# Constant matmuls in two of TensorE's gaps, and ScalarE's weight copy behind the second root at four layer boundaries

## The chip, the cores and the metric

One core of a Trainium2 chip runs the kernel. The metric is the device time of one execution in microseconds. Engines are named as in the profile: PE is TensorE (PEld its weight loads), DVE VectorE, ACT ScalarE, POOL GpSimd, SP SyncE, which issues the DMAs.

## What is computed

Three layers run over 512 tokens of 1024 features, all in float32. The first is a convolution block: two projections around a gated depthwise convolution of 31 taps and a layer norm. The second is latent attention with 8 heads. The third mixes a gated delta rule and a sliding window. Each is followed by a feed-forward part. The part of the reference that matters here is what stands between two parts, in the first two layers:

```python
for layer in range(DEPTH):
    ...
    h = h + rms_norm(m, mix_post_g[layer])
    f = squared_relu_mlp(rms_norm(h, ffn_pre_g[layer]), w_ff1[layer], w_ff2[layer])
    h = h + rms_norm(f, ffn_post_g[layer])
```

So between two projections stand a norm of the output, an addition to the residual, and a second norm. And in the convolution block:

```python
u = jax.nn.silu(layer_norm(u, ln_g, ln_b))
return u @ w_pw2 + b_pw2
```

## The kernel before

Features lie on the 128 partitions, the 512 tokens along the free axis; 1024 features are 8 tiles. Every engine has its own list of instructions, written out by hand, and runs it in that order; semaphores connect them. Nothing is scheduled by a planner.

**Weights** come as a stream of numbered chunks of 128 x 2048 float32. For chunk c SP loads `wraw`, ACT copies it to `whi` in a rounded form (`head(c)`, line 626), and the rest `wlo = wraw - whi` is made either by POOL (`rest(c)`, line 535) or, for the chunks named in `BY_DVE`, by VectorE (`weights_low(c)`, line 1279). Activations are split the same way into a high part (`xh`, `hh`) and a low part (`xl`, `hl`). A projection then takes three matmuls in place of one: high x high, high x low, low x high (line 2113 for 512 columns, line 2136 for half the tokens, 256 columns). TensorE starts chunk c when `lo_ready` has reached c + 1 and the pair of PSUM banks is free. SP loads chunk c when `lo_ready` has reached c - 1.

**The beginning.** ACT squares the input, VectorE adds the squares up, TensorE sums them over the partitions with a matmul of ones (line 2204), ACT makes the root (lines 641 and 642), and VectorE and ACT make `xh` and `xl` tile by tile (lines 1266, 654, 1259), for which TensorE waits. In the convolution block POOL adds products of taps (line 542), VectorE adds others (line 1437), TensorE others (`taps`, line 2227), and a sigmoid gate (ACT line 769, VectorE line 1416) stands before each tile's taps.

**The layer norm ahead of the second projection** (`pw2`): TensorE sums tiles and squares (lines 2249 and 2254), then ACT and VectorE make the root, SiLU, `hh` (line 827) and `hl` (line 1514) tile by tile. The projection takes each tile as it comes.

**A boundary** (`boundary(i, ...)` on PE, DVE and ACT, for i = MIX0, FFN0, MIX1, FFN1; the fifth boundary, OUT, has code of its own) joins the last four chunks of one part (the last is `last`) and the first two of the next (`last + 1`, `last + 2`). The tokens are taken in two halves, so that the second half's projection hides the first half's norms. TensorE's order is: chunks last-1 and last for half 0, the same for half 1, then last+1 and last+2 for half 0, then both for half 1. Within chunk last+1, half 0, after its first four operand tiles, it does the last sums of squares of half 1:

```python
project_half(last + 1, half, hi, lo, need=need(0, half),
             midway=((0, 4), lambda: post_sums(i, 1, (3, 4))) if half == 0 else None)
```

These sums wait for ACT's last square `post_square(3, 1)` (line 668), which waits for VectorE's evacuation `evac(3, 1)` (line 1536, 1540 or 1581). The sums release ACT's root `post_root_of(1)` (Ln on line 673, Exp on 674). `high(0, j, half)` (line 679) makes the high part of the next operand, `low` (line 1304) on VectorE the low part, after `scale` (line 1293) and `add` (line 1299). VectorE's order around chunk last+2 is:

```python
for j in range(4, DT):
    low(0, j, 0)
weights_low(last + 2)
if i == FFN0:
    for j in range(DT):
        low(1, j, 0)
dve.wait_ge(post_root, 2 * i + 2)
```

and behind it come the scales, additions and low parts of half 1. At FFN0 chunk last+2 has a second operand (`hh`, `hl`). POOL makes the rest of chunk last+3 onwards.

Of the kernel before, what the change touches and what calls it, by code (L numbers as in the profile page):

```python
# [24 lines left out]
P = 128  # L25
# [3 lines left out]
DT = D // P  # L29
# [110 lines left out]
def build(nc, A, out):  # L140
    ctx = ExitStack()
    with ctx:
        def sb(name, shape, dt=F32):
            return ctx.enter_context(nc.sbuf_tensor(name, shape, dt))

        def sem(name):
            return ctx.enter_context(nc.semaphore(name))
# [15 lines left out]
        K = sb("K", [P, N_CONST])  # L163
        PV = sb("PV", [P, N_VEC])
        small = sb("small", [P, N_COLS])
        ps = ctx.enter_context(nc.psum_tensor("ps", [P, 8, SEQ], F32))
# [15 lines left out]
        ident, ones, half_ones = map(const, ("ident", "ones", "half_ones"))  # L182
# [12 lines left out]
        pool_sum, TAP_BANK, ODD_BANK = (E[:, 0, :], E[:, 1, :]), (6, 7), (4, 5)  # L195
# [115 lines left out]
        pair_free = [sem("pair_free_even"), sem("pair_free_odd")]  # L311
# [72 lines left out]
        def weights(c):  # L384

            if c < DT and c // 2 % 2:
                return lent[c % 2][:, 0:CW], lent[c % 2][:, CW:2 * CW]
            return whi[:, c % 2, :], wlo[:, c % 2, :]

        def weights_free(eng, c, h=0):  # L390

            if c >= DT + 2:
                eng.wait_ge(chunk_done, h * 2 + (c - 1))
            elif c >= 4:
                eng.wait_ge(chunk_done, c - 3)

        def pair(c):
            return 2 * (c % 2)
# [5 lines left out]
        def emptied(eng, c, h=0):  # L404

            eng.wait_ge(pair_free[c % 2], h + (c // 2 + 1))
# [202 lines left out]
        def _(act):  # L609
            steps = [0]  # L610

            def step(ins):

                steps[0] += 1
                ins.then_inc(act_step, 1)
                act.wait_ge(act_step, steps[0])

            def head(c, h=0):

                if isinstance(h, int) and c + 2 * h >= N_CHUNK:  # L620
                    return
                p = c % 2
                w = WIDTH[c + 2 * h] if isinstance(h, int) else CW
                act.wait_ge(raw_loaded[p], h * 16 + 16 * (c // 2 + 1))
                weights_free(act, c, h)
                act.activation(weights(c)[0][:, 0:w], wraw[:, p, 0:w], ACT.Copy).then_inc(hi_ready, 1)  # L626
# [32 lines left out]
            def boundary(i):  # L659
                last = LAST[i]  # L660

                def post_square(m, half):
                    if half:
                        emptied(act, last - 3 + m)
                    else:
                        act.wait_ge(evac_half, 2 * i + m - 1)
                    s = 2 * (m - 2)
                    act.activation(sq_half[:, s:s + 2, :], Y[:, 2 * m:2 * m + 2, TOK[half]],
                                   ACT.Square).then_inc(post_sq, 1)

                def post_root_of(half):
                    act.wait_ge(post_summed, 2 * i + half + 1)
                    step(act.activation(POST[half], POST[half], ACT.Ln, scale=1.0 / D, bias=eps_rms))
                    act.activation(POST[half], POST[half], ACT.Exp, scale=-0.5).then_inc(post_root, 1)

                def high(s, j, half):
                    (name, at, hi, _), hi_sem, _, _ = pre_norms(i)[s]
                    act.wait_ge(resid_half, DT * i + DT // 2 * half + j // 2 + 1)
                    act.activation(hi[:, j, TOK[half]], resid[:, j, TOK[half]], ACT.Copy,
                                   scale=vec(name, at + j)).then_inc(hi_sem, 1)  # L680

                def pre_squares(half):
                    for m in range(DT // 2):
                        act.wait_ge(resid_half, DT * i + DT // 2 * half + m + 1)
                        act.activation(Z[:, 2 * m:2 * m + 2, TOK[half]], resid[:, 2 * m:2 * m + 2, TOK[half]],
                                       ACT.Square).then_inc(pre_sq, 1)

                for m in range(2):
                    c = last - 3 + m
                    head(c + 2)  # L690
                    emptied(act, c)
                    if m:
                        act.wait_ge(post_added, 3 * i + 1)
                    for n in range(2):
                        act.activation(SQ[:, n, :], Y[:, 2 * m + n, :], ACT.Square).then_inc(post_sq, 1)
                    if m == 0 and i == MIX0:
                        act.wait_ge(rel_summed, 1)
                        act.activation(rel_rows, ps[0:SW_H, 6, 0:RELW], ACT.Copy).then_inc(rel_copied, 1)
                act.wait_ge(post_added, 3 * i + 2)
                post_square(2, 0)  # L700
                post_square(3, 0)
                post_root_of(0)
                head(last + 1)
                post_square(2, 1)
                for j in range(6):
                    high(0, j, 0)
                head(last + 2)
                post_square(3, 1)
                for j in range(6, DT):
                    high(0, j, 0)  # L710
                post_root_of(1)
                if i == FFN0:
                    for j in range(DT):
                        high(1, j, 0)
                pre_squares(0)
                for j in range(DT):
                    high(0, j, 1)
                if i == FFN0:
                    for j in range(DT):
                        high(1, j, 1)  # L720
                    head(last + 3)
                pre_squares(1)
# [34 lines left out]
            c0 = START["pw1"]  # L757
# [72 lines left out]
            c0 = START["pw2"]  # L830
# [39 lines left out]
            c0 = START["latent"]  # L870
# [233 lines left out]
            for t in range(TT):  # L1104
                par = t % 2
                act.wait_ge(rows_summed, t + 1)
                c0 = COLS["state_decay"][0] + 8 * par
# [962 lines left out]
        def _(pe):  # L2070
# [19 lines left out]
            def project(c, hi, lo, h=0, k_tiles=DT, k0=0, need=None, second=None, second_need=None,  # L2090
                        paired=True, midway=None, hooks={}, start=True, bank=None):

                if start:
                    start_chunk(c, h)
                p = c % 2
                bank = 2 * p if bank is None else bank

                order = ([(n, k) for k in range(k_tiles) for n in range(2)] if need and paired else
                         [(n, k) for n in range(2) for k in range(k_tiles)])
                for n, k in order:  # L2100
                    if midway and (n, k) == (1, 0):
                        midway()
                    if (n, k) in hooks:
                        hooks[(n, k)]()
                    if n and second:
                        hi, lo = second
                    if need and n == 0:
                        need(k)
                    if second_need and n == 1:
                        second_need(k)  # L2110
                    w = slice(k * 2 * P + n * P, k * 2 * P + (n + 1) * P)
                    for q, (wt, xt) in enumerate(passes(hi, lo, *weights(c))):
                        ins = pe.matmul(ps[:, bank + n, :], wt[:, w], xt[:, k0 + k, :],  # L2113
                                        start=k == 0 and q == 0, stop=k == k_tiles - 1 and q == 2)
                    if isinstance(h, int) and c == N_CHUNK - 1 and (n, k) == (0, k_tiles - 1):
                        ins.then_inc(last_half, 1)
                ins.then_inc(chunk_done, 1)
# [64 lines left out]
            def operand(name):  # L2182
                return lambda k: pe.wait_ge(split_done, SPLIT0[name] + k + 1)

            def project_tokens(c, k_tiles, n_out, need=None, hooks={}):
# [13 lines left out]
                                            start=k == 0 and q == 0, stop=k == k_tiles - 1 and q == 2)  # L2199
                ins.then_inc(chunk_done, 1)  # L2200

            pe.wait_ge(ones_loaded, 16)
            pe.wait_ge(squares_added, 1)
            pe.matmul(ps[:, SUMS, :], ones, Y[:, 0, :], start=True, stop=True).then_inc(squares_summed, DT)
            c0 = START["pw1"]
            ready = operand("mix0_pre")

# [57 lines left out]
            rest_sum(DT - 1).then_inc(rest_summed, 1)  # L2265
            rest_square(DT - 1)
            c0 = START["pw2"]
            project(c0, hh, hl, need=operand("ln"))

            def distance_bias():  # L2270
# [9 lines left out]
            def ffn(layer):  # L2280
# [11 lines left out]
                with pe.Fori(1, FF_BLOCKS - 1) as b:  # L2292
# [12 lines left out]
                    bank=LATENT_BANK)  # L2305
# [281 lines left out]
            for t in range(TT):  # L2587
# [40 lines left out]
                for lv in range(1, 6):  # L2628
# [4 lines left out]
                    for g in range(2):  # L2633
                        pe.wait_ge(level_x, 10 * t + 2 * lv + g - 1)
                        for i in range(2):
# [3 lines left out]
                                            start=True, stop=True)  # L2639
# [11 lines left out]
                    for g in range(2):  # L2651
# [3 lines left out]
                        for i in range(2):  # L2655
                            hp = slice((2 * g + i) * P, (2 * g + i + 1) * P)
                            ip, up = slice(i * P, (i + 1) * P), slice(HALF + i * P, HALF + (i + 1) * P)
                            if lv < 5:
                                ins = pe.matmul(ps[:, LEVEL_Q[g], ip], inverse[g][:, up], level_mask[:, hp],  # L2659
                                                start=True, stop=True)  # L2660
                            else:
                                ins = pe.matmul(ps[:, LEVEL_Q[g], up], level_mask[:, hp], inverse[g][:, up],
                                                start=True, stop=True)
# [201 lines left out]
```

## Time and profile before

| | |
|---|---|
| median of 3 runs | 1952.64 us (1952.09 to 1953.35) |
| the profiled execution's own time | 1951.87 us |
| its span, first to last instruction | 1950.1 us |
| mean granted TensorE clock | 0.999 |
| busy: PE, PEld | 1909.4 us (98%), 1592.3 us (82%) |
| busy: DVE, ACT, POOL | 824.0, 783.3, 681.5 us |
| the longest line: L2113 on PE | 61% of the chain that ended last |

Matmuls are pipelined, so a record's duration is longer than the distance to the next: one counts distances between starts. A float32 matmul has two records (a matmul of rounded operands one). The chain that ended last is followed back from the last instruction; what is on it sets the end. The four boundaries lie around 190 to 242, 546 to 603, 754 to 807 and 1111 to 1163 us.

### The profile page before, as it was taken

The page shows a single profiled execution, that of the slowest core. Times are in us where ns is not written, and L with a number is a line of the kernel's source. Part 1 is how long each engine was busy: PE and PEld are TensorE (multiplying, and loading weights), DVE is VectorE, ACT ScalarE, POOL GpSimd, SP SyncE. Part 2 cuts the span into 40 slices and gives each one's busy share as a digit, 9 for nine tenths or more (in the row PEclk, how much of TensorE's full clock was granted, in tenths as well). Part 3 has the DMA queues.
Part 4 walks back from the last instruction along what each step waited for, and adds up shares of the span by engine and source line. Part 5 has one row for each costly group of instructions (what it writes and reads, how often), then busy time and mean ns, then how long its engine had stood idle before and what let it go on. Part 6 is the DMA issues. An engine that isn't in the chain of part 4 may idle for free.

```text
span 1950.1 us, 24716 instructions
## 1 busy us (share of the span) xinstructions
PE 1909.4 (98%) x9804; PEld 1592.3 (82%) x9804; DVE 824.0 (42%) x1366; ACT 783.3 (40%) x1179; POOL 681.5 (35%) x217
## 2 busy tenths in 40 slices
PE   6998999999999999999999999999999999999999
PEld 4666988888897779888888897778898898888887
DVE  5996621111266474612111377756552352122122
ACT  6665432222345462523222256755454342122221
POOL 3993043434301210243343313222123403434442
PEclk9999999999999999999999999999999999999999
DMA  5211264222221211332322312111122322222322
GB/s 191 68 42 66 76 122 102 101 89 105 89 90 49 81 44 47 106 108 87 108 104 90 108 56 87 66 49 60 44 82 92 114 82 107 96 99 87 108 81 92
DMA packets 30510, 169.40 MB, mean 87 GB/s; under 512 B 3755, under 2 KB 6092, under 8 KB 13516
## 3 DMA queue, kind: packets, MB, share of 16 engines
q1 hardware_dynamic: 30412, 168.01, 25.8%
q8 instruction: 72, 1.18, 0.3%
q14 instruction: 26, 0.21, 0.0%
HBM read 162.22 MB, written 5.77 MB: 86 GB/s over the span
## 4 chain that ended last, share of the span: by engine, by line
PE 88%; DVE 5%; ACT 4%; POOL 2%; issue 1%; DMA 1%; SPq 0%; POOLq 0%; DVEq 0%; ACTq 0%
PE ps L2113 61%; PE ps L2136 8%; PE ps L2474 4%; PE ps L2541 3%; PE ps L2227 2%; POOL wlo L535 1%; PE ps L2638 1%; PE ps L2198 1%; ACT whi L626 1%; PE ps L2659 1%; DVE wlo L1279 1%; PE ps L2363 1%; PE ps L2380 1%; PE ps L2381 1%; PE ps L2398 1%
## 5 line engine op out<-in xcount | busy, mean ns | idle before, releaser
L535 POOL TENSOR_TENSOR wlo<-wraw,whi 128x2048 fp32r<-128x2048 f32 (+4 forms) x138 | 570.5, 4134 | 1192.1 <-ACT whi L626 1160.3
L626 ACT ACTIVATE whi<-wraw 128x2048 fp32r<-128x2048 f32 (+4 forms) x154 | 268.1, 1741 | 372.1 <-PE ps L2113 348.8
L2113 PE MATMUL ps<-xh,whi 128*128 128x512 f32 x980 | 386.7, 395 | 5.8 <-DVE xl L1259 4.3
L2113 PE MATMUL ps<-xl,whi 128*128 128x512 f32 x980 | 382.0, 390 | 0.0
L2113 PE MATMUL ps<-xh,wlo 128*128 128x512 f32 x980 | 381.9, 390 | 0.0
L2113 PE MATMUL ps<-hh,whi 128*128 128x512 f32 x752 | 295.3, 393 | 5.9 <-DVE hl L1514 5.7
L2113 PE MATMUL ps<-hh,wlo 128*128 128x512 f32 x752 | 293.1, 390 | 0.0
L2113 PE MATMUL ps<-hl,whi 128*128 128x512 f32 x752 | 293.1, 390 | 0.0
L2113 PEld LDWEIGHTS ps<-xh,whi 128*128 128x128 f32 x980 | 184.4, 188 | 48.3 <-issue 8.7
L2113 PEld LDWEIGHTS ps<-xl,whi 128*128 128x128 f32 x980 | 184.4, 188 | 39.3 <-issue 1.9
L2113 PEld LDWEIGHTS ps<-xh,wlo 128*128 128x128 f32 x980 | 184.3, 188 | 38.5
L2113 PEld LDWEIGHTS ps<-hh,whi 128*128 128x128 f32 x752 | 141.5, 188 | 37.7 <-issue 8.5
L2113 PEld LDWEIGHTS ps<-hl,whi 128*128 128x128 f32 x752 | 141.6, 188 | 30.0 <-issue 1.0
L2113 PEld LDWEIGHTS ps<-hh,wlo 128*128 128x128 f32 x752 | 141.4, 188 | 29.6
L848 ACT ACTIVATE hh<-Z 128x1024 fp32r<-128x1024 f32 x32 | 33.9, 1059 | 214.7 <-DVE Z L1560 212.0
L1560 DVE SCALAR_TENSOR_TENSOR Z<-ps,RS 128x1024 f32<-128x1024 f32 x28 | 34.3, 1224 | 183.2 <-PE ps L2113 183.2
L1437 DVE SCALAR_TENSOR_TENSOR ps<-Z,PV,ps 128x512 f32<-128x512 f32 x140 | 96.2, 751 | 8.4 <-ACT ps L801 4.1
L2136 PE MATMUL ps<-hh,whi 128*128 128x256 f32 x336 | 97.8, 291 | 0.0
L2136 PE MATMUL ps<-hh,wlo 128*128 128x256 f32 x336 | 95.1, 283 | 0.0
L2136 PE MATMUL ps<-hl,whi 128*128 128x256 f32 x336 | 95.0, 283 | 0.0
L2136 PE MATMUL ps<-xh,whi 128*128 128x256 f32 x304 | 88.1, 290 | 1.6 <-DVE xl L1304 1.6
L2136 PE MATMUL ps<-xl,whi 128*128 128x256 f32 x304 | 86.0, 283 | 0.0
(351 smaller groups left out, 2958.0 us busy)
## 6 DMA issues: line engine op xcount, KB each, us to landing
wraw<-stream SPq DMA_DIRECT2D x132, 1024.0 KB, 4.8
wraw<-stream SPq DMA_DIRECT2D x12, 768.0 KB, 4.1
wraw<-stream SPq DMA_DIRECT2D x6, 384.0 KB, 3.2
resid<-x SPq DMA_DIRECT2D x4, 512.0 KB, 5.1
wraw<-stream SPq DMA_DIRECT2D x8, 256.0 KB, 3.0
branch_scratch<-RS SPq DMA_DIRECT2D x8, 256.0 KB, 2.0
wraw<-stream SPq DMA_DIRECT2D x4, 512.0 KB, 3.7
rel_scratch<-E SPq DMA_DIRECT2D x8, 192.0 KB, 8.9
```

The source lines that it names most:

```text
L535: pool.tensor_tensor(lo[:, 0:w], wraw[:, p, 0:w], hi[:, 0:w], ALU.subtract).then_inc(lo_ready, 1)
L626: act.activation(weights(c)[0][:, 0:w], wraw[:, p, 0:w], ACT.Copy).then_inc(hi_ready, 1)
L848: act.activation(hh[:, 2 * j:2 * j + 2, :], t, ACT.Square)
L1279: dve.tensor_tensor(wlo[:, p, 0:w], wraw[:, p, 0:w], whi[:, p, 0:w], ALU.subtract).then_inc(lo_ready, 1)
L1437: dve.scalar_tensor_tensor(out=NT[:, at:at + 1, :] if last else acc, in0=x, scalar=tap(k, j, h), in1=acc, op0=ALU.mult, op1=ALU.add).then_ ...
L1560: ins = dve.scalar_tensor_tensor(out=t, in0=ps[:, 2 * p:2 * p + 2, :], scalar=0.0, in1=rs_pair(), op0=ALU.max, op1=ALU.mult)
L2113: ins = pe.matmul(ps[:, bank + n, :], wt[:, w], xt[:, k0 + k, :], start=k == 0 and q == 0, stop=k == k_tiles - 1 and q == 2)
L2136: ins = pe.matmul(half_bank(c, half)[:, n, :], wt[:, p, w], xt[:, k, TOK[half]], start=(n, k, q) == (0, 0, 0), stop=(n, k, q) == (1, DT - ...
L2198: ins = pe.matmul(dst, xt[:, k, t * P:(t + 1) * P], wt[:, p, k * n_out:(k + 1) * n_out], start=k == 0 and q == 0, stop=k == k_tiles - 1 an ...
L2227: ins = pe.matmul(ps[:, TAP_BANK[at], :], w, shifted(k, j, h), start=n == 0, stop=n == len(diags) - 1)
L2474: ins = pe.matmul(ps[:, slot_bank(s), :], wt[:, c % 2, w], xt[:, m // 3, :], start=m == 0, stop=m == 3 * DT - 1)
L2541: ins = pe.matmul(ps[:, bank, :], wt[:, p, w0 + k * P:w0 + (k + 1) * P], xt[:, k0 + k, :], start=r in (0, 24), stop=r == last)
```

## The change

1. In ACT's `boundary`, `head(last + 2)`, which stood between the high parts 0 to 5 of half 0 and `post_square(3, 1)`, now stands behind that square, the high parts 6 and 7 and `post_root_of(1)`. This holds for all four boundaries.
2. On TensorE a new function `stay_awake` multiplies the identity by 256 columns of constants in float32, into a bank that nobody reads at the time: six times behind the first sum (bank 7), eleven times ahead of the second projection (the first bank of its pair, which the projection's own start overwrites). Ahead of the eleven stands a wait that the projection had anyway (`pair_free[0]`).

```diff
                 post_square(2, 1)
                 for j in range(6):
                     high(0, j, 0)
-                head(last + 2)
                 post_square(3, 1)
                 for j in range(6, DT):
                     high(0, j, 0)
                 post_root_of(1)
+                head(last + 2)
                 if i == FFN0:
                     for j in range(DT):
                         high(1, j, 0)
...
+            def stay_awake(bank, times):
+
+                for n in range(times):
+                    pe.matmul(ps[:, bank, 0:2 * P], ident, K[:, 0:2 * P], start=True, stop=True)
+
             pe.wait_ge(ones_loaded, 16)
             pe.wait_ge(squares_added, 1)
             pe.matmul(ps[:, SUMS, :], ones, Y[:, 0, :], start=True, stop=True).then_inc(squares_summed, DT)
+            stay_awake(TAP_BANK[1], 6)
             c0 = START["pw1"]
...
             rest_sum(DT - 1).then_inc(rest_summed, 1)
             rest_square(DT - 1)
             c0 = START["pw2"]
+            pe.wait_ge(pair_free[0], DT // 2)
+            stay_awake(pair(c0), 11)
             project(c0, hh, hl, need=operand("ln"))
```

ACT's order at the first boundary (L626 is the weight copy, L668 the square, L679 the high parts, L673 and L674 the root, L685 squares for the next norm):

```order
 L668 ACTIVATE SQ<-Y 128x512
 L679 ACTIVATE xh<-resid,PV 128x256 x6
-L626 ACTIVATE whi<-wraw 128x2048
 L668 ACTIVATE SQ<-Y 128x512
 L679 ACTIVATE xh<-resid,PV 128x256 x2
 L673 ACTIVATE ps<-ps,small 128x256
 L674 ACTIVATE ps<-ps 128x256
+L626 ACTIVATE whi<-wraw 128x2048
 L685 ACTIVATE Z<-resid 128x2x256 x4
 L679 ACTIVATE xh<-resid,PV 128x256 x8
```

The copy went past five instructions; the order on VectorE, POOL and SP is the same as before.

TensorE's order ahead of the second projection, before (L2249 and L2254 are the sums, L2113 the projection):

```order
L2249 MATMUL ps<-Y,K 128x512
L2254 MATMUL ps<-SQ,K 128x512
L2249 MATMUL ps<-Y,K 128x512
L2254 MATMUL ps<-SQ,K 128x512
L2113 MATMUL ps<-hh,whi 128x512
L2113 MATMUL ps<-hl,whi 128x512
```

and in the changed kernel (the same sums are lines 2255 and 2260 there):

```order
L2255 MATMUL ps<-Y,K 128x512
L2260 MATMUL ps<-SQ,K 128x512
L2205 MATMUL ps<-K 128x256 x11
L2113 MATMUL ps<-hh,whi 128x512
L2113 MATMUL ps<-hl,whi 128x512
```

The eleven constant matmuls stand between the last sum and the projection's first matmul, which waits for the first `hl`.

## Rows read from the trace of the kernel before

**Rows 1.** The page: the chain that ended last, by engine.
```profile
PE 88%; DVE 5%; ACT 4%; POOL 2%; issue 1%; DMA 1%; SPq 0%; POOLq 0%; DVEq 0%; ACTq 0%
```
**Rows 2.** Waits of PE, whole run: line, released by: us in total, times, longest.
```profile
PE ps L2113 <- DVE hl L1514: 5.7, 1, 5.7
...
PE ps L2150 <- ACT SQ L668: 2.6, 4, 0.8
```
**Rows 3.** The chain in order of time, first 240 us: start, us, what.
```profile
33.18 4.55 POOL hh L535
...
49.77 3.67 PE ps L2227 x8
```
**Rows 4.** PE in order of time, the beginning: start, us, what, [idle before <-releaser].
```profile
18.22 0.77 PE L2113 MATMUL ps<-xh,whi 128*128 128x512 f32 x1 [4.33 <-DVE xl L1259]
...
34.53 3.67 PE L2227 MATMUL ps<-Z 128*128 128x512 f32 x8 [0.88 <-DVE Z L1416]
```
**Rows 5.** Stretches around the second gap: length, busy us of each engine, then PEclk.
```profile
162.20:164.40 2.20, 0.00 (x0) 0.00 (x0) 1.44 (x3) 2.16 (x4) 2.20 (x3) 1.00 0.88 372
164.40:165.30 0.90, 0.00 (x0) 0.01 (x1) 0.82 (x2) 0.87 (x3) 0.48 (x1) 0.77 0.04 18
165.30:168.30 3.00, 2.98 (x7) 2.42 (x8) 2.72 (x5) 2.32 (x4) 0.00 (x0) 0.50 0.00 0
```
**Rows 6.** PE in order of time, the second projection.
```profile
165.32 0.77 PE L2113 MATMUL ps<-hh,whi 128*128 128x512 f32 x1 [5.72 <-DVE hl L1514]
...
168.39 0.39 PE L2113 MATMUL ps<-hl,whi 128*128 128x512 f32 x1
...
177.47 0.39 PE L2113 MATMUL ps<-hh,wlo 128*128 128x512 f32 x1
```
**Rows 7.** The chain: two float32 matmuls of 256 columns (four records).
```profile
204.61 0.87 PE ps L2150 x4
```
**Rows 8.** DVE in order of time: the first and the last of the eight hl.
```profile
164.48 0.69 DVE L1514 TENSOR_TENSOR hl<-ps,hh 128x512 fp32r<-128x512 f32 x1 [0.84 <-ACT hh L827]
...
174.69 0.69 DVE L1514 TENSOR_TENSOR hl<-ps,hh 128x512 fp32r<-128x512 f32 x1 [0.61 <-ACT hh L827]
```
**Rows 9.** ACT in order of time, first boundary.
```profile
216.60 1.90 ACT L626 ACTIVATE whi<-wraw 128x2048 fp32r<-128x2048 f32 x1
218.40 0.61 ACT L668 ACTIVATE SQ<-Y 128x512 f32<-128x512 f32 x1
218.92 0.89 ACT L679 ACTIVATE xh<-resid,PV 128x256 fp32r<-128x256 f32 x2
220.24 0.45 ACT L673 ACTIVATE ps<-ps,small 128x256 f32<-128x256 f32 x1 [0.42 <-PE ps L2150]
...
221.00 2.18 ACT L685 ACTIVATE Z<-resid 128x512 f32<-128x512 f32 x4
```
**Rows 10.** DVE in order of time, first boundary.
```profile
216.47 0.87 DVE L1536 TENSOR_SCALAR Y<-ps,PV 128x256 f32<-128x256 f32 x2
...
218.15 0.69 DVE L1299 TENSOR_TENSOR resid<-resid,Y 128x512 f32<-128x512 f32 x1
...
220.34 2.29 DVE L1279 TENSOR_TENSOR wlo<-wraw,whi 128x2048 fp32r<-128x2048 f32 x1
```
**Rows 11.** PE, first boundary: the sums, and the first matmul of chunk last+2.
```profile
219.07 1.13 PE L2150 MATMUL ps<-SQ,K 128*128 128x256 f32 x4 [0.80 <-ACT SQ L668]
...
222.90 0.28 PE L2136 MATMUL ps<-xh,whi 128*128 128x256 f32 x1
```
**Rows 12.** ACT's second Ln and DVE's low part of chunk last+2, second boundary.
```profile
576.62 0.45 ACT L673 ACTIVATE ps<-ps,small 128x256 f32<-128x256 f32 x1 [0.42 <-PE ps L2150]
...
576.63 2.28 DVE L1279 TENSOR_TENSOR wlo<-wraw,whi 128x2048 fp32r<-128x2048 f32 x1
```
**Rows 13.** PE, second boundary: first matmul of chunk last+2, and a later wait.
```profile
579.29 0.28 PE L2136 MATMUL ps<-xh,whi 128*128 128x256 f32 x1
...
590.16 0.39 PE L2136 MATMUL ps<-xh,whi 128*128 128x256 f32 x1 [0.61 <-DVE xl L1304]
```

## The prediction

> **What bounds the kernel now.** I read the page's chain by engine first, then TensorE's list of waits, then the order in time around the places that the change touches. The chain by engine says that TensorE is the bound nearly everywhere: it has 88% of it [rows 1]. So a microsecond is won or lost only where TensorE stands still or runs slowly. Its list of waits is short. The two entries that bear on this change are the 5.7 us ahead of the second convolution projection (waiting for hl) and 2.6 us in four pieces, all before the sums of the squares at a boundary (L2150, waiting for ACT's square at L668) [rows 2].
>
> **Constants in the first gap: nothing.** Six fp32 matmuls of 256 columns now stand between the first sum and the first projection. TensorE waited 4.33 us there, and the projection began at 18.22 us [rows 4]. Two such matmuls took 0.87 us at the full clock, so 0.435 each [rows 7]; at half clock 0.87 each, 5.2 us in all. The first sum ended 4.33 before 18.22, at 13.9, so at worst the six end near 19.1, 0.9 us after the projection could have begun. At best they raise the clock early and the first chunk ends some 0.7 us sooner. Neither reaches the end of the kernel: the chain there does not run over TensorE but over ACT and POOL (POOL's weight rest at 33.18 us and its products) and joins TensorE only at 49.77 us [rows 3], and TensorE itself still stands 0.88 us before its first taps at 34.53, for VectorE's gate [rows 4]. That gate comes after an ACT sigmoid that stands behind ACT's tap weights and weight copy. I take 0, with bounds of -0.7 and +0.1.
>
> **Constants in the second gap: a gain of 0.7 us.** After the last sum of squares TensorE is idle for 5.72 us and begins the projection at 165.32 [rows 6]. The granted clock was 1.00 from 162.2 to 164.4, 0.77 from 164.4 to 165.3, and 0.50 from 165.3 to 168.3: it fell near the end of the idle stretch from 2.4 to 1.2 GHz [rows 5]. The first seven matmuls took 3.07 us (165.32 to 168.39) and the next forty are 0.227 apart (168.39 to 177.47) [rows 6], so slowness cost 3.07 - 7 x 0.227 = 1.5 us. Now eleven constant matmuls fill 11 x 0.435 = 4.8 us; the last sum had ended at 165.32 - 5.72 = 159.6, so they are through at 164.4, 0.9 us before the first hl is there. They delay nothing, and an idle stretch of 0.9 us is less than the 4.8 us that passed at full clock. The whole 1.5 is not won, because ACT and VectorE hand over hl tile by tile: the last one begins at 174.69 and takes 0.69, so it is there at 175.38. The first was there at 165.17 (164.48 + 0.69) [rows 8], and TensorE began at 165.32: a handover of 0.15. So the last tile's six matmuls (6 x 0.227 = 1.36) start at 175.5 at the earliest and end at 176.9, against 177.47 + 0.23 = 177.7 before. That is 0.8; a restart after a short wait costs some 0.1, so I take 0.7. Bounds: 0 (the clock falls all the same) and 1.5. Everything behind hangs on this projection, so the gain carries on.
>
> The Trainium skill (TensorE: Matmul & The Clock Gate, "Part 1: The HAM clock gate") says that the number of slow matmuls varies between runs of one kernel, with 6 to 14 measured. This trace shows 7; with the rule's upper figure the gain would be up to 1.4 us larger and the sum +5.5 instead of +6.9. I go by the trace.
>
> **The weight copy at the four boundaries: a loss of 7.6 us.** In each boundary ACT's copy for chunk last+2 (1.90 us) moves behind the second half's last square, the last two high parts and the second root. I follow the first boundary.
>
> Before: copy at 216.60, square at 218.40, high parts at 218.92, Ln at 220.24, and the instruction behind Ln and Exp at 221.00, 0.76 after Ln [rows 9]. TensorE stood 0.80 us for that square, until 219.07 [rows 11].
>
> Now: VectorE's last evacuation ends at 217.34 (216.47 + 0.87) [rows 10], so the square runs at 217.37. TensorE gets to its sums at 218.27 and does not stand: 0.80 won there. High parts 6 and 7 need VectorE's addition, which ends at 218.84 (218.15 + 0.69) [rows 10]; their 0.89 less the usual overlap of 0.08 keeps ACT until 219.68. The sums, 0.80 earlier, release Ln from 219.44 (219.07 to 220.24 was 1.17). So Ln is at 219.68, and the copy starts at 220.44 and ends at 222.34.
>
> What is late next: VectorE's own order is unchanged, and it wanted this copy at 220.34 for the low part of chunk last+2, 2.29 us long [rows 10]. It now stands until 222.37, **2.03 us**, and behind it on VectorE stand all the scales, additions and low parts of the second half. The low part is ready at 222.37 + 2.29 = 224.66, and TensorE needs 0.15 from there. Before, TensorE took up that chunk at 222.90 [rows 11], 0.27 after the low part was there (222.63). So it has only 0.12 us of cover: it arrives 0.8 earlier, waits some 2.6, and begins at 224.8, **1.9 us later** than before. The 0.80 won is already inside this.
>
> The other three boundaries have the same rows with a wait of 0.61 instead of 0.80 ((2.6 - 0.8) / 3 from rows 2). There the sums, not the high parts, release Ln, so it comes 0.61 earlier, and the copy ends at old Ln - 0.61 + 0.76 + 1.90, which is 2.05 after the old Ln. VectorE wanted it 0.01 after the old Ln (576.63 against 576.62) [rows 12], so with a 0.03 handover it is 2.07 late. TensorE's cover is 579.29 - 578.91 - 0.15 = 0.23 [rows 12, 13], so 1.8 later at the second of the feed-forward boundaries and at the attention's. At the first feed-forward boundary TensorE afterwards stood three times for VectorE's low parts (the last 0.61 us at 590.16) [rows 13]; it is VectorE's delay that counts there: 2.07.
>
> ACT's queue: behind the copy stand the squares of the sum and the second half's high parts, which wait for VectorE's additions anyway and are later by what VectorE is later. SP's load of chunk last+4 waits for the same low part, so its DMA is issued 2 us later; its copy comes only after chunks that are later by as much. POOL works on chunk last+3 onwards, off the same TensorE signal as before.
>
> Sum: 1.9 + 2.07 + 1.8 + 1.8 = 7.6, less 0.7, is +6.9. The profiled execution took 1951.87 us (span 1950.1), so 1958.8; the median of the runs shown, 1952.64, is 0.77 above that execution, so I say **1959.5 us**. Its own range is 1957.3 to 1961.9: 0.3 for each boundary, the bounds of the second gap, and 0.7 of scatter.
>
> **Rivals.**
> (a) *The clock falls in the new waits.* TensorE now stands some 2.6 us at each boundary. If that takes the clock to half, each boundary pays what the slow stretch above cost, 1.5 us, four times: 1965.4. Against it: the clock was still 1.00 at 162.2 to 164.4, after more than 2.6 us without a matmul [rows 5]. The Trainium skill (same page, "A second HAM failure mode: psum-queue depth-cycling") has a kernel in which even small repeated idle stretches let the clock swing; in this trace TensorE stood 0.80 us before 219.07 and then did two sums and 24 matmuls of 256 columns in the 3.83 us to 222.90 [rows 11], while seven of 512 columns took 3.07 us at half clock, so the trace does not show that here. 7%.
> (b) *The copy is covered after all.* If VectorE's or TensorE's next need for chunk last+2 lay more than 2 us behind, the change would win all waits: 0.7 + 0.8 + 3 x 0.61 = 3.3, giving 1949.3. That decides at a cover of 2.0 us; the rows show VectorE with none and TensorE with 0.12 to 0.23. 6%.
> (c) *The boundary loses, but half.* If the copy ran about 1 us earlier than I work out (ACT waiting less for the sums, or the 1.90 us overlapping what stands ahead), each boundary would lose 1 us: 1952.64 + 4 - 0.7 = 1955.9. 5%.
> (d) *The constants do nothing for the clock.* Then the sum is +7.6, inside my range. It is part of the forecast.
> The forecast itself has 80%; 2% is left for what I have not thought of.
>
> **How the numbers follow.** A measurement of this kernel tells about 0.2% (3.9 us) from no change, so slower means above 1956.5. The forecast and (a) lie there: 0.87. Rivals (b) and (c) are no change: 0.11. Faster by over 0.2% needs more than all waits won: 0.02. The range runs from 1957.0 to 1964.0: the forecast's own, and above it a clock that falls in one or two of the boundaries.
>
> **What the next profile would show.** TensorE's list of waits: no entry for L2150 behind ACT's square, and in its place four of some 2.6 us at the first matmul of chunk last+2, released by VectorE's wlo at L1279. VectorE: that instruction preceded by about 2 us of idle time on ACT's whi. Before the second projection: about 0.9 us idle instead of 5.72, granted clock 1.00 behind it. Its first matmul is no earlier than before. I am wrong if VectorE does not stand there, if TensorE takes chunk last+2 up without a wait, or if the granted clock behind a boundary's wait reads 0.50.

## The result, and the profile after

| | before | after |
|---|---|---|
| median | 1953.34 us (1952.09 to 1953.97, 6 runs) | 1961.42 us (1959.27 to 1962.12, 6 runs) |
| ratio, 95% interval | | 1.0041 [1.0031, 1.0051] |
| profiled execution: its time, span | 1951.87, 1950.1 us | 1959.27, 1957.5 us |
| VectorE, ScalarE, POOL busy | 824.0, 783.3, 681.5 us | 823.8, 784.1, 681.6 us |

The change costs 8.1 us. The three engines beside TensorE do as much work as before, and the span is 7.4 us longer, so the time is TensorE's, standing still or running slowly. TensorE's list of waits in the changed kernel (line, released by: us in total, times, longest) says where:

```profile
PE ps L2136 <- DVE wlo L1279: 9.2, 4, 2.3
...
PE ps L2136 <- DVE xl L1304: 1.8, 3, 0.6
PE ps L2113 <- DVE hl L1514: 1.0, 1, 1.0
```

The entry of the square at the boundaries [rows 2] is gone, and in its place stand four waits of 2.3 us for VectorE's low part of the weights. The wait before the second projection went from 5.7 to 1.0 us, because constants fill the rest.

ScalarE in order of time at the first boundary (to be held against [rows 9]):

```profile
214.47 0.91 ACT L679 ACTIVATE xh<-resid,PV 128x256 fp32r<-128x256 f32 x2 [3.30 <-DVE resid L1299]
216.04 0.63 ACT L668 ACTIVATE SQ<-Y 128x512 f32<-128x512 f32 x1 [0.67 <-DVE Y L1536]
217.55 0.91 ACT L679 ACTIVATE xh<-resid,PV 128x256 fp32r<-128x256 f32 x2 [0.87 <-DVE resid L1299]
218.36 0.42 ACT L673 ACTIVATE ps<-ps,small 128x256 f32<-128x256 f32 x1
218.82 0.37 ACT L674 ACTIVATE ps<-ps 128x256 f32<-128x256 f32 x1
219.10 1.91 ACT L626 ACTIVATE whi<-wraw 128x2048 fp32r<-128x2048 f32 x1
```

VectorE there [rows 10], the last low parts of the operand and then the low part of the weights:

```profile
217.43 1.67 DVE L1304 SCALAR_TENSOR_TENSOR xl<-resid,PV,xh 128x256 fp32r<-128x256 f32 x4
221.04 2.29 DVE L1279 TENSOR_TENSOR wlo<-wraw,whi 128x2048 fp32r<-128x2048 f32 x1 [1.94 <-ACT whi L626]
```

And TensorE [rows 11, 13], the first matmul of chunk last+2 at the four boundaries:

```profile
223.39 0.38 PE L2136 MATMUL ps<-xh,whi 128*128 128x256 f32 x1 [2.29 <-DVE wlo L1279]
...
581.48 0.38 PE L2136 MATMUL ps<-xh,whi 128*128 128x256 f32 x1 [2.29 <-DVE wlo L1279]
...
791.85 0.51 PE L2136 MATMUL ps<-xh,whi 128*128 128x256 f32 x1 [2.29 <-DVE wlo L1279]
...
1151.41 0.38 PE L2136 MATMUL ps<-hh,whi 128*128 128x256 f32 x1 [2.29 <-DVE wlo L1279]
```

ScalarE's copy starts 0.74 us after Ln. VectorE had nothing that it might do first and stood 1.94 us. TensorE stood 2.29.

**Where 7.4 us come from.** I take the distances between the same points of the two profiles. From the start of the second projection to the first boundary's chunk last+2: 57.58 us before (165.32 to 222.90), 58.70 after (164.69 to 223.39), +1.1. To the last wait of the second boundary: 367.26 before (to 590.16), 369.27 after (592.66), +2.0. To the third boundary's chunk: 197.58 before (787.74), 199.19 after, +1.6. To the fourth's: 356.40 before (1144.14), 359.56 after, +3.2. That is 7.9. The changed kernel's profile was 0.6 ahead already where the second projection begins (164.69 against 165.32), and 0.1 came at the end. Two of these points in the profile of before:

```profile
787.74 0.28 PE L2136 MATMUL ps<-xh,whi 128*128 128x256 f32 x1
...
1144.14 0.28 PE L2136 MATMUL ps<-hh,whi 128*128 128x256 f32 x1
```

and the last wait of the second boundary after:

```profile
592.66 0.39 PE L2136 MATMUL ps<-xh,whi 128*128 128x256 f32 x1 [0.60 <-DVE xl L1304]
```

The odd one is the last, which holds 3.2 where the same wait cost 1.6 to 2.0 elsewhere (1.8 at the first boundary, without the 0.7 of the constants). The stretches of 3.0 us behind the four waits (length, busy us of each engine, then PEclk):

```profile
223.40:226.40 3.00, 3.00 (x25) 3.00 (x26) 2.93 (x7) 0.93 (x3) 0.00 (x0) 1.00 0.60 180
581.50:584.50 3.00, 3.00 (x25) 3.00 (x26) 3.00 (x8) 2.87 (x6) 0.00 (x0) 1.00 0.32 87
791.90:794.90 3.00, 3.00 (x14) 3.00 (x15) 2.93 (x7) 0.97 (x3) 0.00 (x0) 0.51 0.62 191
1151.40:1154.40 3.00, 2.99 (x25) 2.99 (x26) 2.93 (x7) 0.91 (x2) 0.00 (x0) 1.00 0.52 177
```

Behind the third wait TensorE ran at 0.51 of its clock, 1.2 GHz, and did 14 matmuls where it did 25 behind the others: 11 x 0.12 = 1.3 us lost in this window; the clock came back only at about 795.4, which makes it 1.5. So my rival (a) happened as well, at one boundary of this execution. How often it happens is what the experiments settle.

### The profile page after: what moved, and what is told of

Read it like the earlier page. It is cut to its first block, busy times and chain, and to the rows that moved or that the text cites. A ratio compares the mean times of both kernels' runs of the same rounds, so it can differ in the third digit from the quotient of the medians.

```text
span 1957.5 us, 24784 instructions
## 1 busy us (share of the span) xinstructions
PE 1918.3 (98%) x9838; PEld 1598.4 (82%) x9838; DVE 823.8 (42%) x1366; ACT 784.1 (40%) x1179; POOL 681.6 (35%) x217
## 4 chain that ended last, share of the span: by engine, by line
PE 87%; DVE 6%; ACT 4%; POOL 2%; issue 1%; DMA 0%; SPq 0%; POOLq 0%; DVEq 0%; ACTq 0%
PE ps L2113 61%; PE ps L2136 8%; PE ps L2482 4%; PE ps L2549 3%; PE ps L2233 2%; POOL wlo L535 1%; DVE wlo L1279 1%; ACT whi L626 1%; PE ps L2646 1%; PE ps L2198 1%; PE ps L2667 1%; PE ps L2371 1%; DVE Y L1293 1%; PE ps L2388 1%; PE ps L2389 1%
## 5 line engine op out<-in xcount | busy, mean ns | idle before, releaser
L626 ACT ACTIVATE whi<-wraw 128x2048 fp32r<-128x2048 f32 (+4 forms) x154 | 268.2, 1741 | 372.3 <-PE ps L2113 348.1
L2113 PE MATMUL ps<-xh,whi 128*128 128x512 f32 x980 | 386.4, 394 | 1.8 <-POOL wlo L535 0.8
L2113 PE MATMUL ps<-xh,wlo 128*128 128x512 f32 x980 | 381.5, 389 | 0.0
L2113 PE MATMUL ps<-xl,whi 128*128 128x512 f32 x980 | 381.5, 389 | 0.0
L2113 PE MATMUL ps<-hh,whi 128*128 128x512 f32 x752 | 294.8, 392 | 1.2 <-DVE hl L1514 1.0
L2113 PE MATMUL ps<-hh,wlo 128*128 128x512 f32 x752 | 292.7, 389 | 0.0
L2113 PE MATMUL ps<-hl,whi 128*128 128x512 f32 x752 | 292.7, 389 | 0.0
L2113 PEld LDWEIGHTS ps<-xh,whi 128*128 128x128 f32 x980 | 184.0, 188 | 43.8 <-issue 3.0
L2113 PEld LDWEIGHTS ps<-xl,whi 128*128 128x128 f32 x980 | 184.0, 188 | 39.0 <-issue 1.9
L2113 PEld LDWEIGHTS ps<-xh,wlo 128*128 128x128 f32 x980 | 183.9, 188 | 38.6
L2113 PEld LDWEIGHTS ps<-hh,whi 128*128 128x128 f32 x752 | 141.1, 188 | 33.4 <-issue 3.3
L2113 PEld LDWEIGHTS ps<-hl,whi 128*128 128x128 f32 x752 | 141.2, 188 | 29.8 <-issue 1.0
L2113 PEld LDWEIGHTS ps<-hh,wlo 128*128 128x128 f32 x752 | 141.1, 188 | 29.5
```

## The experiments

My theory: the loss is the time by which the copy is late for VectorE, and on top of it the clock, where it falls in TensorE's new waits. Rivals: the constants cost something themselves; it is the delayed square or root that counts and not the copy; and the excess over my sum is VectorE and not the clock. The first four kernels shared one chip (before: 1952.65 us, 23 runs), the next four another (before: 1952.19 us, 21 runs). Each result is to be read against its own before.

### The new order alone

```diff
-            stay_awake(TAP_BANK[1], 6)
...
             pe.wait_ge(pair_free[0], DT // 2)
-            stay_awake(pair(c0), 11)
```

> The change without its seventeen constant matmuls: only ScalarE's copy for chunk last+2 stands behind the second root, at all four boundaries. My theory (VectorE wants that copy at once and stands about 2.0 us for it, TensorE has 0.1 to 0.2 us of cover): four entries of 2.3 us in TensorE's list of waits behind VectorE's wlo, +7.4 us, and on top 1.4 us for each boundary in which the clock falls during the wait: 1960.7 to 1963.5 us against 1953.3. Rival (the constants cost something themselves, and the order costs less): 1957 us or below.

1962.41 us (1959.71 to 1963.43), ratio 1.0047 [1.0034, 1.0061]: 9.8 us slower than before. The order loses, in the medians more than with the constants in. The same four stretches in its profile, and the one behind the start of the second projection:

```profile
224.30:227.30 3.00, 3.00 (x20) 3.00 (x21) 2.93 (x7) 0.97 (x3) 0.00 (x0) 0.74 0.61 191
583.90:586.90 3.00, 3.00 (x15) 3.00 (x16) 3.00 (x8) 2.86 (x6) 0.00 (x0) 0.54 0.34 93
794.20:797.20 3.00, 3.00 (x19) 3.00 (x20) 2.93 (x7) 0.91 (x2) 0.00 (x0) 0.76 0.57 180
1153.90:1156.90 3.00, 3.00 (x15) 3.00 (x16) 2.93 (x7) 0.96 (x3) 0.00 (x0) 0.54 0.54 178
164.90:168.00 3.10, 3.08 (x8) 2.48 (x9) 2.82 (x5) 2.42 (x4) 0.00 (x0) 0.55 0.00 0
```

In this execution the clock was down behind all four waits, in the changed kernel's profile behind one. The waits are the same 2.28 to 2.29 us, so a wait of this length may or may not cost the clock. And it fell behind the wait, not in it. At the first boundary TensorE was back at work from 224.24 us:

```profile
224.30:225.70 1.40, 1.40 (x12) 1.40 (x13) 1.37 (x4) 0.00 (x0) 0.00 (x0) 1.00 0.31 47
...
225.80:229.00 3.20, 3.20 (x18) 3.20 (x17) 3.13 (x8) 1.75 (x4) 0.00 (x0) 0.50 1.02 332
```

It worked 1.5 us at full clock before the clock went to half. Read in steps of 0.2 us, the other four falls of these two profiles come 0.1 to 1.6 us after TensorE's restart.

### The constants alone, and the eleven alone

```diff
                     high(0, j, 0)
+                head(last + 2)
                 post_square(3, 1)
                 for j in range(6, DT):
                     high(0, j, 0)
                 post_root_of(1)
-                head(last + 2)
```

> The change without its new ScalarE order: only the six and the eleven constant matmuls. Theory: the six are worth nothing, the eleven 0.77 us (the second projection ends that much earlier against its start): 1952.5 us. Rival (the 0.6 us that the changed kernel was ahead already at its first taps comes from the six constants and not from when the first weights landed): 1951.9 us. A second rival, constants in TensorE's way: above 1953.3.

1951.09 us (1950.26 to 1953.14, 11 runs), ratio 0.9992 [0.9983, 1.0001]: 1.6 us faster by the medians. The second kernel in addition leaves out `stay_awake(TAP_BANK[1], 6)`.

> Only the eleven constants ahead of the second projection. Theory: 1952.5 us, the same as with both sets within 0.2 us; the first projection then starts again with seven or eight matmuls 0.43 apart, and the first taps are no later for it. Rival (the six are worth 0.6 us): 0.6 us slower than with both sets, 1953.1.

1951.25 us (1950.42 to 1952.64, 11 runs), ratio 0.9994 [0.9985, 1.0003]. With and without the six constants the medians lie 0.16 us apart, so the six are worth nothing that can be measured. The first kernel's median came nearer to the rival's 1951.9 than to my 1952.5, but the second refutes the rival. The 0.6 us by which the changed kernel's profile was ahead is scatter: ScalarE's first weight copy, which waits for its DMA, began at 13.65 us in before and at 12.06 in the changed kernel, and the new order without constants was 0.4 ahead too (second projection at 164.92). The eleven are worth 1.4 us in medians, twice the 0.7 that I took. Neither interval excludes no change, but the mean granted clock of each run shows what happens. It was 1.000 in 10 of the 11 runs with the eleven constants alone. In the 23 runs of before it was 0.998 in nineteen, 0.999 in three and 0.997 in one. The one profile that I worked from was such a 0.999, with 3.4 us at half clock (164.9 to 168.3); a 0.998, rounded as it is, stands for 5.9 to 9.8 us. The two kernels differ in nothing but the gap ahead of the second projection, so that is where the time at half clock lies. It costs more than in the trace in most runs: those nineteen have a median of 1952.68 us, the three at 0.999 1952.06, the one at 0.997 1954.31.

### Four more constants in each new wait

```diff
+                    if half == 0:
+                        pe.wait_ge(pair_free[(last + 2) % 2], (last + 2) // 2)
+                        stay_awake(pair(last + 2) + 1, 4)
                     project_half(last + 2, half, hi, lo, second=sets[1][0][2:] if two else None,
```

> The changed kernel with four more constant matmuls of 256 columns (1.7 us) between the two chunks of half 0 in each boundary, where TensorE now waits about 2.3 us for VectorE. Theory (what the changed kernel takes over my sum is the clock, which falls in some of these waits): the waits shrink to about 0.6 us without an earlier end, no stretch behind them is at 0.50, and the median falls from 1961.4 to 1959.2 us with less scatter between runs. Rival (the excess is something else, VectorE being later than worked out): 1961.4 as before, or above it if the constants are in the way.

1958.30 us (1957.84 to 1958.74, 7 runs), ratio 1.0030 [1.0019, 1.0042]. The granted clock is 1.0 in all seven runs, and the range between runs is 0.9 us, where it was 2.9 for the change. TensorE's waits:

```profile
PE ps L2136 <- DVE wlo L1279: 2.2, 4, 0.6
```

TensorE is busy with constants and still starts the chunk when VectorE lets it, at 223.31 us in the first boundary, where it was 223.39. Against its own before this kernel is 5.65 us slower, and the change 8.1: the clock in the waits costs 2.4 us in the median, at 1.5 a time between one and two boundaries out of four. The intervals of the two ratios overlap; the times do not (the slowest of these seven is 1958.74, the fastest of the change's six 1959.27), and neither do the clock readings, 1.000 in all seven against 0.998 or 0.999 in the six. Against the constants alone it is 1958.30 - 1951.09 = **7.2 us** slower, and that is the price of the new order with the clock kept out of it. The two profiles say the same without the scatter of the beginning: from the start of the second projection to the end of the span it is 1956.1 - 164.63 = 1791.5 us here and 1949.1 - 164.90 = 1784.2 with the constants alone, 7.3 apart. The four distances of above are +1.1, +2.1, +1.6 and +1.7 in this profile: the fourth, 3.2 in the change, has lost its 1.5 of slow clock.

### The copy one place earlier

```diff
+                head(last + 2)
                 post_root_of(1)
-                head(last + 2)
```

> The changed kernel with ScalarE's copy one place earlier: behind the square and the high parts 6 and 7, ahead of the second root. My theory is that each boundary loses what the copy is later for VectorE. It now starts at the end of the high parts, 0.76 us earlier than in the change at the first boundary and 0.9 us earlier at the others, so VectorE stands about 1.2 us instead of 2.0, TensorE waits some 1.4 us, and the four cost 1.1 + 1.2 + 0.9 + 0.9 = 4.1 us, less 0.7 for the constants: 1956.1 us against 1952.7. With waits that short I expect the clock to stay up. Rival (it is the delayed square, or the root, that TensorE pays for and not the copy): no better than the change, 1961 us.

1955.26 us (1954.45 to 1956.08, 11 runs), ratio 1.0015 [1.0006, 1.0024]. The four waits are 1.54 us long instead of 2.29, the clock is 1.0 in all runs, and the loss is 3.1 us where I expected 3.4 (4.1 for the order, less 0.7). With the 1.4 to 1.6 that the constants give, the order itself costs 4.5 to 4.6. The root is now later than in the change and the square as early as there, so neither is what TensorE pays for: the copy is.

### The copy later still

```diff
-                head(last + 2)
                 if i == FFN0:
                     for j in range(DT):
                         high(1, j, 0)
                 pre_squares(0)
+                head(last + 2)
```

> A dose: the changed kernel with ScalarE's copy still later, behind the four squares of the sum of half 0 (2.0 us), and at the first feed-forward boundary behind the eight high parts of the second operand as well (3.2 us). Theory: each boundary is later by just that, 3 x 2.0 + 5.2 = 11.2 us over the changed kernel, and the waits of over 4 us take the clock down at all four where before it fell in about two: 1972 to 1976 us. Rival (part of the delay is absorbed by slack behind the chunk): clearly less than 11 us more than the change.

1974.25 us (1973.93 to 1976.15, 4 runs), ratio 1.0116 [1.0100, 1.0131]. The first matmuls of chunk last+2 at the first and second boundary:

```profile
225.58 0.39 PE L2136 MATMUL ps<-xh,whi 128*128 128x256 f32 x1 [4.37 <-DVE wlo L1279]
...
590.44 0.58 PE L2136 MATMUL ps<-xh,whi 128*128 128x256 f32 x1 [7.55 <-DVE wlo L1279]
```

Waits of 4.4 and 7.6 us, 2.1 and 5.3 more than in the change, as the instructions that ScalarE does first would have it. The time is 22.1 us over its before against 8.1: 14.0 more, where I expected 11.2 and the clock. Of the 14.0, 11.5 are longer waits (2.08, 5.26, 2.07 and 2.06). The rest is put down to the clock, which is at 0.993 to 0.996 in the mean and at 0.50 behind all four waits of the profile. (The three waits for xl at the second boundary, 1.8 us in the change, are gone there: behind a fall of the clock TensorE comes to them later. They take up a part of what the clock costs.) The delay of the copy comes out in full, so no slack behind the chunk absorbs it.

### The copy earlier than before

ScalarE stood 3.3 us ahead of the high parts 4 and 5. The chunk's buffer comes free at about the time at which these could begin.

```diff
-                for j in range(6):
+                for j in range(4):
                     high(0, j, 0)
+                head(last + 2)
                 post_square(3, 1)
-                for j in range(6, DT):
+                for j in range(4, DT):
                     high(0, j, 0)
                 post_root_of(1)
-                head(last + 2)
```

> The changed kernel with ScalarE's copy moved the other way: ahead of the high parts 4 and 5, where ScalarE stood 3.3 us idle; the chunk's buffer comes free at the same moment, so it ends near 217.2 us at the first boundary, before the square can run. Theory: VectorE never stands for it, TensorE's wait for the square (0.80 and 0.61 us) goes, but of that only 0.1 to 0.2 us counts at each boundary, since VectorE's low part of the chunk ends when it did before: 0.5 us in all with 0.7 for the constants, 1951.4 us. Rival (the wait for the square was a true loss): 0.8 + 3 x 0.61 + 0.7, 1949.3 us.

1950.27 us (1949.85 to 1950.74, 11 runs), ratio 0.9990 [0.9981, 0.9999]: the only version with an interval that lies below 1. The wait for the square is gone, and 0.26 us remain at each chunk last+2:

```profile
221.93 0.39 PE L2136 MATMUL ps<-xh,whi 128*128 128x256 f32 x1 [0.26 <-DVE wlo L1279]
```

Of its 1.9 us the constants give 1.4 to 1.6 by the two kernels without the new order (on the other chip), so the order gives 0.4 to 0.5; by the distance from the second projection to the end of the span (1948.6 - 165.23 = 1783.4 against 1784.2) it gives 0.8. Either is far from the 2.6 us of the four waits for the square, as my theory had it: VectorE, not ScalarE, sets when the chunk can start. It carries the cause of the boundary's length one step further: VectorE has no idle time there to give.

### VectorE's part given to POOL

In addition to the last kernel, POOL makes the low part of chunk last+2 at the four boundaries.

```diff
-BY_DVE = {c + i for c in LAST for i in range(3)} | ...
+BY_DVE = {c + i for c in LAST for i in range(3 if c == LAST[-1] else 2)} | ...
...
+                if isinstance(h, int) and c - 2 in LAST[:-1]:
+                    pool.wait_ge(lo_ready, c)
                 weights_free(pool, c, h)
...
-                weights_low(last + 2)
                 if i == FFN0:
```

> copy_early with the low part of chunk last+2 made by POOL (4.6 us, idle there) instead of VectorE (2.29 us) at the four boundaries. Theory (VectorE's queue is what holds the boundary): POOL ends near 221.8 us at the first one, before TensorE gets there at 222.1; the waits for the square are won in full (0.8 + 3 x 0.61), and at the first feed-forward boundary also the three waits for VectorE's low parts (1.6 us): 4.2 and 0.7 for the constants, 1947.8 us. Rival (VectorE and POOL slow each other when both run, or POOL is late): TensorE waits for POOL's wlo and the time is 1950 us or above.

1969.13 us (1967.92 to 1971.12, 5 runs), ratio 1.0087 [1.0074, 1.0101], where I expected 1947.8: my theory of this kernel fell. POOL was in time, and TensorE did not wait for it at a boundary. POOL at the first boundary:

```profile
216.64 4.53 POOL L537 TENSOR_TENSOR wlo<-wraw,whi 128x2048 fp32r<-128x2048 f32 x1 [32.92 <-ACT whi L628]
```

and VectorE at the same time (L1301 is the addition to the residual, L1299 in the other kernels):

```profile
216.40 0.86 DVE L1295 SCALAR_TENSOR_TENSOR Y<-Y,PV,ps 128x256 f32<-128x256 f32 x2
217.30 4.43 DVE L1301 TENSOR_TENSOR resid<-resid,Y 128x512 f32<-128x512 f32 x1
221.65 1.66 DVE L1306 SCALAR_TENSOR_TENSOR xl<-resid,PV,xh 128x256 fp32r<-128x256 f32 x4
```

An addition that takes 0.69 us elsewhere took 4.43. It began 0.66 us after POOL's subtraction and ended 0.56 after it. Everything behind it on VectorE was late, so TensorE stood 3.9 us at each boundary, four times, with the clock down behind it. The Trainium skill (SBUF — State Buffer, Who interferes with whom) says that a VectorE instruction with two SBUF inputs contends with a GpSimd instruction that reads SBUF, and that of the two the later one is held up until the other is done. By that rule the addition, with 216.64 + 4.53 = 221.17 us as the end of POOL's subtraction, could not end before it; the trace agrees, it ended at 221.73. The rival that I wrote down came near, but as a mutual slowing, at 1950 us or above, and with TensorE waiting for POOL. The rows show POOL's subtraction at its usual length (4.53 us) and one VectorE instruction that stands until it is done.

## Why the prediction was right or wrong

The direction and the mechanism held. I said 1959.5 with a range of 1957.0 to 1964.0; measured were 1961.42. Against the median of its own before the sum was +6.9 and the measurement is +8.1. That is close in part by luck. The waits' clock, put at nothing, cost 2.4; against it stood 0.8 that the constants gave beyond my 0.7, and 0.4 by which the order was cheaper. And of my three signs of being wrong one came true: the granted clock behind the third boundary's wait read 0.51 in the window shown, 0.50 within it.

- **Constants in the first gap, 0.** Held: 1951.09 with them and 1951.25 without. With them the first projection's matmuls are 0.23 us apart from the start, where they were 0.43 in before; nobody waits for it. (PEclk reads 1.00 there in both, so this slow start is not in the mean clocks.)
- **Constants in the second gap, -0.7.** Right for the trace I had: from the second projection's start to the first boundary's chunk last+2 the kernel with the constants alone takes 56.94 us (164.90 to 221.84) and before 57.58, so -0.64. Too small in the median: -1.4 to -1.6. The term was mis-sized at the price of the half clock, which I took from the one profile. Its 3.4 us at half clock were the short case; most runs of before show 0.998 in the mean and not 0.999. The sentence of the Trainium skill (TensorE: Matmul & The Clock Gate, Part 1) on six to fourteen slow matmuls, which I quoted and set aside, gave -2.1 as an upper estimate; the runs' -1.4 to -1.6 lie between it and the trace's -0.7.
- **The first boundary, +1.9.** The rows show +1.1 with the constants' share of -0.7 in it, so +1.8. VectorE stood 1.94 us against 2.03.
- **The other three, +2.07, +1.8 and +1.8.** +2.0, +1.6 and, with the clock kept up, +1.7. The new order's own price came to 7.2 us (four more constants in each wait against the constants alone) where I had 7.6.
- **The cover.** I gave VectorE none and TensorE 0.12 to 0.23 us, because I took 0.15 for the handover. In the change it is 0.06 (the low part is there at 221.04 + 2.29 = 223.33, the chunk starts at 223.39), so the cover is 0.09 more at each boundary, most of the 0.4 between 7.6 and 7.2. The doses bear the rest out: waits of 1.54, 2.29 and 4.37 us (7.55 at the first feed-forward boundary) for the three places behind the high parts, with losses of 3.1, 8.1 and 22.1 us.
- **Rival (a), the clock falls in the new waits, 7%.** Far too low. It fell at one boundary in the profiled execution and cost 2.4 us in the median. I argued that the clock was still up after 2.6 us of idle [rows 5]. That reading looked at the wrong place: the clock was read inside an idle stretch, and behind the waits of 2.3 us it fell up to 1.6 us after TensorE was at work again. A clock of 1.00 during an idle stretch does not show that the stretch costs none. With waits of 1.54 us the mean clock read 1.000 in all of 11 runs, with waits of 0.55 us in all of 7; waits of 2.29 us cost it in some places and not in others of the same execution.
- **Rivals (b) and (c)**, the copy covered or half covered: excluded by the waits of 2.29 us.
- **Rival (d)**, constants that do nothing: excluded, since the granted clock is 1.0 with them.

The corrected terms, 7.2 + 2.4 - 1.5, add up to 8.1, but as differences of the same medians they must; what checks them apart from the medians are the 7.3 us between two profiles, the 1.5 us of one slow stretch, and the clock readings of the runs.

## What to carry to other kernels

Before an instruction is moved back on one engine, look at what the receiving engine does in the instruction before it wants the result: here the gain of 0.8 us was visible in TensorE's list of waits and the price of 2.0 was not in any list, because the copy had always been in time. Here, in a chain of three engines, the one without idle time (VectorE) decided, and freeing ScalarE won a few tenths. And an idle stretch's price in clock is to be taken from the mean granted clock of many runs, and from the rows behind the stretch, not from one trace and not from the rows inside it.

## What the runs showed that I had not expected

- The clock may fall after a wait of 2.29 us, and in these two profiles it did so only when TensorE was back at work: behind four waits of that length it was down once in one execution, four times in another, each time 0.1 to 1.6 us after the restart. Ahead of the second projection of before it stayed up for 5.3 us of idle time and fell 0.4 us before the restart. Filling 1.7 of the 2.3 us with constants kept it up in all of seven runs and took the range between runs from 2.9 to 0.9 us. On what it depends which wait is hit these runs do not show.
- A VectorE addition of two SBUF tensors (128x512, float32, 0.69 us) that starts while POOL subtracts two SBUF tensors takes until POOL is done: 4.43 us. The kernel before has it already, and TensorE does not wait for it: at the start of each of the four boundaries an addition on L1314 takes 4.16 to 4.18 us beside POOL's weight rest, where the same line takes 0.68 without it.
- In most runs of before the gap ahead of the second projection costs more time at half clock (5.9 to 9.8 us by a mean of 0.998) than its profile shows (3.4).
